# Input projection of a hybrid decoder step: Strassen's seven products in place of the direct one, with the sums of weight blocks formed on GpSimd

## The chip, the core and the metric

The kernel runs on one core of a Trainium2 chip. A core has TensorE (matmuls, out of SBUF into PSUM), VectorE, ScalarE, GpSimd, SyncE (which here only issues DMAs) and 16 DMA engines. The metric is the device time of one execution in microseconds. The engines run their own instruction lists in order and meet at semaphores.

## The reference

One step of a decoder layer, for a prompt of 1024 tokens and 8 samples of 4 tokens (1056 tokens in all). What the change touches is the first line of the layer:

```python
h = rmsnorm(x, norm_g) * (1 + scale[:, None, :]) + shift[:, None, :]
u = h @ w_in        # 1056 x 1024  by  1024 x 6960
# q (1024 columns), three K/V pairs and gates (816), conv h, B, C (1024 each), z (2048)
```

The columns for q, h, B, C and the two halves of z, 6144 of them, are the "input projection" below. From them come `u = cc * hc`, `y_conv = bc * short_conv(u)`, times `silu(z_c)`; `silu(z_a)`; and q. The K/V columns go to the compressed, selected and window attention. Everything is fp32; each fp32 product is made of three products of rounded parts (high x high, high x low, low x high).

## The kernel before

**Stages.** TensorE's list is: the modulation vectors from ada_w (`L997`); the key/value columns, for the samples (`kv_sample`) and then for each of 8 prompt tiles of 128 tokens (`kv(s)`, `L989` to `L991`, 48 matmuls of 384 and 432 columns each); the input projection (`project`, `L1025`); the compression of cached and new keys and values (`turn`, `pair`: transposes `L1069` to `L1071` and matmuls `L1077`, a first pass for keys and a second for values); attention; the output projection (`L1386`).

**The input projection before.** The 6144 columns are 8 groups j of 6 kinds (CC, HC, BC, ZC, ZA, QQ), each 128 columns wide, 48 column groups. The weights wr (1024 x 128, 512 KB) of a group are split by ScalarE into a rounded high part wh (`L1470`) and by VectorE into the low rest wl (`L1775`); the tokens were split once into hhi and hlo (`L1764`). A group is 8 slices of the inner dimension x 3 products (wh hhi, wh hlo, wl hhi) x 3 column chunks of 352 tokens: 72 matmuls, each with its own 128 x 128 weight load, into three PSUM banks; the kinds alternate between two sets of three. ScalarE and VectorE evacuate (cct, uu, yy, zt, ych, zab, qhi, qlo), GpSimd stores mixed, z_attn_silu and q_stacked.

**Order around it.** Every engine's list is written out by hand. SyncE (`load_w`) loads wr two kinds ahead. Before its first load it waits for the store of the bias rows (`row_st`, `L513`, 3 MB). Between the loads stand, one at a time, those for the gate vector (gw, 8 x 512 KB, `L545`, `L548`, `L564`), for the compression's weights (w1, `load_w1`, `L528`, in j = 3) and for the rows of new keys (xp, `load_rows`, `L535` and `L537`, 24 DMAs in j = 4 to 7). The gate products (`gates`, `L1033`) stand between the first kinds. Behind the projection SyncE issues `load_rows(1, r)`, 24 DMAs for the values, and `load_w1(1, q)`. GpSimd gathers the cached keys in quarters of 2 MB (`gather_quarter`, `L781`): the first before the projection, the second right behind it, the others after the last stores and the memset `L814`. `turn(0, 0)` waits for the first quarter and for all 24 row loads (`xp_ld[c]` at 384).

Of the kernel before, what the change touches and what calls it, by code (L numbers as in the profile page):

```python
# [45 lines left out]
NK = 6  # L46
# [11 lines left out]
def build(nc: "bass.Bass", x_prompt, x_sample, cache_k_cmp, cache_v_cmp, cache_k_slc, cache_v_slc, cache_k_win,  # L58
# [27 lines left out]
    with ctx:  # L86
# [3 lines left out]
        zad = nc.dram_tensor("z_attn_silu", [8, P, TOK], F32, kind="Internal").ap()  # L90
        mixd = nc.dram_tensor("mixed", [16, P, TOK], F32, kind="Internal").ap()
# [11 lines left out]
        idxc = sb("idxc", [P, 2], I32)  # L103
        idxq = sb("idxq", [P, 2, 4], I32)
        idxs = sb("idxs", [P, NB], I32)
        pidx = sb("pidx", [P, 2], I32)
        pgc = sb("pgc", [P, 2], I32)
        pgs = sb("pgs", [P, NB], I32)
        sg = sb("sg", [P, NTT, 3 * NH])
        kcs = sb("kcs", [P, NB * NSB])  # L110
        vcs = sb("vcs", [NSB, NB, DKV])
        kcp = sb("kcp", [P, NG, 2 * NPB], F32R)
        sb("apart0", [P, P])
# [4 lines left out]
        kvt = sb("kvt", [P, NTT - 1, KVW], cx=cV)  # L118
# [3 lines left out]

        cH = ExitStack()
        adaw = [sb(f"adaw{i}", [P, 2 * D], cx=cH) for i in range(KC)]
        cH.close()
        cA = ExitStack()
        hhi = sb("hhi", [P, KC, TOK], F32R, cA)
        hlo = sb("hlo", [P, KC, TOK], F32R, cA)

        c0 = ExitStack()  # L130
        vrow = sb("vrow", [31, D], cx=c0)
        relx = sb("relx", [33, NH], cx=c0)
        rel31 = sb("rel31", [32, NH], cx=c0)
# [10 lines left out]
        scale1 = sb("scale1", [P, KC], cx=c0)  # L144
        h32s = sb("h32s", [P, KC, SAMP], cx=c0)
        wkh = [sb(f"wkh{i}", [P, KC, w], F32R, c0) for i, w in enumerate((KV0, KV1))]
        wkl = [sb("wkl0", [P, KC, KV0], F32R, c0)]
        cS = ExitStack()
        adar = sb("adar", [9, 2 * D], cx=cS)
        cS.close()  # L150
        wkl.append(sb("wkl1", [P, KC, KV1], F32R, c0))
        sq = sb("sq", [P, D], cx=c0)
# [2057 lines left out]
```

## Time and profile before

| | |
|---|---|
| median of 3 runs | 1554.61 us (1551.36 to 1560.05) |
| span of the profiled execution | 1556.0 us |
| TensorE busy | 1486.5 us, 96% |
| VectorE, ScalarE, GpSimd busy | 692.7, 621.4, 199.9 us |
| L1025, three kinds of product, 1152 matmuls each | 250.6, 248.3, 248.0 us |
| chain that ended last | TensorE 85% |

The page gives the span of the profiled execution and no time of its own around it. Matmuls overlap, so their busy times exceed the spacing of their starts; what a stage costs is read from the starts. The chain of waits is the work that set the end: a piece of it that becomes shorter shortens the run by as much, until something else is late.

### The profile page before, as it was taken

To read this page: it belongs to the slowest core of one execution; us is meant where nothing else is said; L and a number is where in the kernel's file an instruction comes from. 1 tells how busy PE (TensorE), PEld (TensorE's weight loads), DVE (VectorE), ACT (ScalarE), POOL (GpSimd) and SP (SyncE) were. 2 spreads that over 40 slices of the span, in tenths; PEclk is the share of its full clock that TensorE was granted. 3 is DMA by queue.
4 is the path that set the end of the run, shared out by engine and by line. 5 is a ranking of instruction groups with operands and counts; after the bars stand their busy time and mean duration, and the time that the engine had idled before them with its cause. 6 is when DMAs were issued, how large, how long until landed. Compare 5 with 4: busy or idle time off the path is not lost.

```text
span 1556.0 us, 25222 instructions
## 1 busy us (share of the span) xinstructions
PE 1486.5 (96%) x9878; PEld 1293.1 (83%) x9878; DVE 692.7 (45%) x1790; ACT 621.4 (40%) x1304; POOL 199.9 (13%) x378
## 2 busy tenths in 40 slices
PE   4899999999999999998999998998998999899998
PEld 1799999999999999997777776776776776688886
DVE  2541222323131312216677666666667655653226
ACT  2331111121111111115557777777777765641111
POOL 1100000001102100003011131131131132000000
PEclk8899999999999999999999999999999999999999
DMA  8814343235325243209721121111111019973231
GB/s 334 144 53 164 99 119 96 67 92 125 105 45 163 80 116 86 65 31 312 223 87 30 35 66 42 28 42 42 28 42 42 28 33 362 257 238 95 82 98 35
DMA packets 169061, 164.59 MB, mean 106 GB/s; under 512 B 52780, under 2 KB 150316, under 8 KB 163760
## 3 DMA queue, kind: packets, MB, share of 16 engines
q1 hardware_dynamic: 155136, 97.26, 23.5%
q0 software_dynamic: 13808, 65.73, 12.4%
q8 instruction: 79, 1.29, 0.3%
q14 instruction: 38, 0.31, 0.1%
HBM read 131.27 MB, written 35.83 MB: 107 GB/s over the span
## 4 chain that ended last, share of the span: by engine, by line
PE 85%; DMA 5%; DVE 4%; SPq 3%; ACT 2%; issue 1%; POOL 0%; DVEq 0%; ACTq 0%
PE PS L1025 36%; PE PS L1386 11%; PE PS L1192 8%; PE PS L1157 7%; PE PS L1136 5%; PE PS L1137 3%; PE PS L1077 2%; DMA kb<-in_cache_k_slc,idxs 1%; DMA adaw<-in_ada_w 1%; DMA xb<-in_x_prompt 1%; PE PS L989 1%; PE PS L990 1%; PE PS L991 1%; PE PS L1239 1%; SPq L535 1%
## 5 line engine op out<-in xcount | busy, mean ns | idle before, releaser
L1025 PE MATMUL PS<-hhi,wh 128*128 128x352 f32 x1152 | 250.6, 326 | 0.6 <-ACT kvt L1434 0.6
L1025 PE MATMUL PS<-hhi,wl 128*128 128x352 f32 x1152 | 248.3, 323 | 0.0
L1025 PE MATMUL PS<-hlo,wh 128*128 128x352 f32 x1152 | 248.0, 323 | 0.0
L1025 PEld LDWEIGHTS PS<-hhi,wh 128*128 128x128 f32 x1152 | 195.4, 189 | 4.5 <-issue 3.0
L1556 ACT ACTIVATE pr<-PS,nm 128x640 f32<-128x640 f32 (+7 forms) x256 | 181.2, 709 | 44.5 <-DVE nm L1908 42.1
L1025 PEld LDWEIGHTS PS<-hhi,wl 128*128 128x128 f32 x1152 | 197.8, 188 | 0.0
L1025 PEld LDWEIGHTS PS<-hlo,wh 128*128 128x128 f32 x1152 | 195.6, 188 | 0.0
L1579 ACT ACTIVATE ptt<-PS 128x512 f32<-128x512 f32 x264 | 149.7, 601 | 43.9 <-PE PS L1157 43.6
L1157 PE MATMUL PS<-ident,pr 128*128 128x128 f32 x1056 | 147.4, 274 | 0.0
L1192 PE MATMUL PS<-ptt,kvt 128*64 128x256 f32 x1056 | 137.2, 391 | 0.0
L1775 DVE TENSOR_TENSOR wl<-wr,wh 128x1024 fp32r<-128x1024 f32 x48 | 58.5, 1219 | 168.2 <-ACT wh L1470 167.7
L1157 PEld LDWEIGHTS PS<-ident,pr 128*128 128x128 f32 x1056 | 122.5, 141 | 8.9 <-ACT ptt L1579 0.4
L1470 ACT ACTIVATE wh<-wr 128x1024 fp32r<-128x1024 f32 x48 | 50.6, 1055 | 184.8 <-PE PS L1025 153.5
L1192 PEld LDWEIGHTS PS<-ptt,kvt 128*64 128x64 f32 x1056 | 67.0, 137 | 41.4 <-issue 16.7
L1908 DVE CUSTOM_DVE_ANT_0 PS<-PS,near,nm 128x256 f32<-128x256 f32 x192 | 94.7, 493 | 6.8
L1907 DVE TENSOR_REDUCE nm<-PS 128x1 f32<-128x128 f32 (+5 forms) x128 | 70.5, 551 | 40.1 <-PE PS L1137 39.5
L1136 PE MATMUL PS<-ksh,qb 128*128 128x384 f32 (+3 forms) x192 | 76.6, 401 | 12.0 <-ACT pr L1556 10.5
L1386 PE MATMUL PS<-woh,mh 128*128 128x512 f32 x256 | 79.3, 391 | 0.0
L1386 PE MATMUL PS<-wol,mh 128*128 128x512 f32 x256 | 79.1, 390 | 0.0
L1386 PE MATMUL PS<-woh,ml 128*128 128x512 f32 x256 | 78.8, 389 | 0.0
L1136 PE MATMUL PS<-kwh,qb 128*128 128x384 f32 (+3 forms) x192 | 70.7, 370 | 7.0 <-ACT pr L1556 7.0
L1077 PE MATMUL PS<-xt,w 128*128 128x273 f32 x256 | 72.5, 406 | 4.5 <-DVE xt L1860 3.0
(318 smaller groups left out, 2194.5 us busy)
## 6 DMA issues: line engine op xcount, KB each, us to landing
wr<-in_w_in SPq DMA_DIRECT2D x32, 512.0 KB, 5.9
adaw<-in_ada_w SPq DMA_DIRECT2D x8, 1024.0 KB, 10.1
wr<-in_w_in SPq DMA_DIRECT2D x32, 256.0 KB, 3.8
qb<-q_stacked SPq DMA_DIRECT2D x32, 256.0 KB, 3.1
mr<-mixed SPq DMA_DIRECT2D x16, 512.0 KB, 3.9
mixed<-ych POOLq DMA_DIRECT2D x8, 528.0 KB, 3.4
z_attn_silu<-zab POOLq DMA_DIRECT2D x8, 528.0 KB, 2.9
xb<-in_x_prompt POOLq DMA_DIRECT2D x8, 512.0 KB, 4.8
```

The source lines that it names most:

```text
L1025: ins = pe.matmul(PS[:, bank + c, 0:CH], a[kind % 2][:, k, :], b[:, k, c * CH:(c + 1) * CH], start=(k == 0 and b is hhi and a is wh), stop ...
L1077: ins = pe.matmul(PS[:, 4 + g, 0:CB], w1[c][:, m, :], xt[m // 4 % 2][:, m % 4, g, :], start=(m == 0), stop=(m == 31))
L1136: pe.matmul(PS[:, b0 + c, x:x + m], q, kh[:, g, a:a + m], start=True, stop=False)
L1157: ins = pe.transpose(PS[:, turn_bank(c), h * P:(h + 1) * P], pr[w % 3][:, h, t * P:(t + 1) * P], ident[:, :])
L1192: ins = pe.matmul(PS[64 * g:64 * g + 64, 6, a:a + 2 * P], v, pt[tc % NPT5][:, 2 * g:2 * g + 2, :].rearrange("p j c -> p (j c)"), start=(t ...
L1386: ins = pe.matmul(PS[0:n, b0 + c, :], a[:, k, 0:n], b[k][:, 512 * c:512 * c + 512], start=(k == 0 and a is mh and b is woh), stop=(k == 15 ...
L1470: act.activation(wh[kind % 2][:, :, :], wr[kind % 2][:, :, :], ACT.Copy).then_inc(w_hi, 1)
L1556: act.activation(pr[r][:, h, 0:k], score_cols(b0, w), ACT.Exp, scale=-1.0, bias=nm[:, r, h:h + 1], accum_out=rsum[:, r, h:h + 1]).then_inc ...
L1579: act.activation(pt[tc % NPT5][:, :, :], PS[:, turn_bank(c), :].rearrange("p (h c) -> p h c", h=4), ACT.Copy).then_inc(pt_act, 1)
L1775: dve.tensor_tensor(wl[kind % 2][:, :, :], wr[kind % 2][:, :, :], f32(wh[kind % 2][:, :, :]), ALU.subtract).then_inc(w_lo, 1)
L1907: link(dve.tensor_reduce(low, cols[:, 0:far], AX.X, ALU.min))
L1908: dve.tensor_tensor_reduce(cols[:, far:k], cols[:, far:k], near[:, head_of(u, h), 2 * P - (k - far):2 * P], 1.0, low if far else 3.0e38, A ...
```

## The change

The projection is done in 24 blocks n = 3j + pair; a block has the two kinds of one pair, (CC, HC), (BC, ZC) or (ZA, QQ). The block's product is a 2 x 2 matrix of blocks: the weights are split by kind and by half of the inner dimension, the token matrix by half of the inner dimension and by half of the tokens (H = 528 each). Blocks 0 to 2 are plain, with 8 products; blocks 3 to 23 are "fast", with Strassen's 7. A product is 4 slices x 3 part products x 2 chunks of 264 columns: 24 matmuls (`multiply`).

- The tokens live in `bo[0..6]`, high and low part: four blocks from the start, and five sums, which VectorE (`op_add`, `op_low`), GpSimd (`low_sums`) and ScalarE (`op_high`) form in 20 slices during the plain blocks (PIECES); `bo` 2 and 3 are overwritten by sums at the end.
- The weights: `wr` holds both kinds of a block (2 x 512 KB), loaded when VectorE has made the last low part of the block before. Five of a fast block's seven weight operands are sums or differences of its quarters, formed in fp32 by GpSimd (`added`, 128 x 512, into two buffers wsum), then split by ScalarE (`high`) and VectorE (`low`) into one of five slots wsl. `prepared_at` says at which product which operand is made.
- A fast block's products go through a ring of four PSUM pairs. ScalarE copies products 0 and 1 out; VectorE adds products 2 to 6 onto them (`joined`, two adds each for products 2 to 4).
- The gate products stand in the key/value stage, one behind each tile, with one gw buffer; in front of the first product TensorE waits for ada_ev, VectorE's four additions of gate.
- The compression's w1 and rows are loaded at the end of block 23; the first gather of cached keys starts in block 23, and the second as well. The eight transposes of conv tails come once, behind the projection.
- The layout of z_attn_silu and mixed follows the token halves; q is stored in 8 DMAs per j in place of 4, and mixed and z_attn_silu in 2 each in place of 1.

```diff
+            def multiply(n, k, op, q, first, last):
+                w, b = wsl[(operand0(n) + k) % NSLOT], bo[op]
+                pe.wait_ge(w_lo, operand0(n) + k + 1)
+                for kk in range(HK):
+                    for x, y in ((0, 0), (0, 1), (1, 0)):
+                        for c in range(2):
+                            ins = pe.matmul(PS[:, 2 * q + c, 0:H // 2], w[:, x, kk, :], b[:, y, kk, c * H // 2:(c + 1) * H // 2],
+                                            start=(first and kk == 0 and x == 0 and y == 0), stop=(last and kk == HK - 1 and x == 1))
                 ins.then_inc(p2_mm, 1)
...
             kv_sample()
             for s in range(1, NTT):
                 kv(s)
+                gates(s - 1)
...
+            load_w(0)
+            for k in range(KC):
+                if k:
+                    sp.wait_ge(ada_mm, KC + k)
+                else:
+                    sp.wait_ge(ada_mm, KC)
+                    sp.wait_ge(h_ev, 1)
+                sp.dma_start(gw[:, :], ada3[:, k, 2 * D:3 * D]).then_inc(adaw_ld[k % 4], 16)
+            for n in range(1, NBLK):
+                load_w(n)
+            sp.wait_ge(*made(NBLK - 1, 2))
+            for q in range(4):
+                load_w1(0, q)
+            sp.wait_ge(xz, 1)
+            sp.wait_ge(kc_st, 32)
+            for r in range(4):
+                load_rows(0, r)
...
+            def added(m):
+                n, k = operand_of(m)
+                po.wait_ge(wr_ld, raw_landed(n))
...
+                if sums_to(m) > 2:
+                    po.wait_ge(w_lo, m - 1)
+                po.tensor_tensor(wsum[(sums_to(m) - 1) % 2][:, :, :], raw(*a), raw(*b), op).then_inc(w_sum, 1)
...
+        def prepared_at(n, i):
+            if plain(n):
+                return EARLY_PREP.get((n, i), ())
+            own, following = operand0(n), operand0(n + 1)
+            if i < 3:
+                return (own + 4 + i,)
+            ahead = {5: (following, following + 1), 6: (following + 2, following + 3)}.get(i, ())
+            return ahead if n + 1 < NBLK else ()
```

TensorE at the end of the first prompt tile and the start of the second, before (wkh, wkl: the K/V weights; hhi, hlo: the tokens):

```order
L989 MATMUL PS<-wkh,hhi 128x432
L990 MATMUL PS<-wkl,hhi 128x432
L991 MATMUL PS<-wkh,hlo 128x432
L989 MATMUL PS<-wkh,hhi 128x384 [waits wk_lo,wk_hi,kv_ev,h_lo,h_hi]
L990 MATMUL PS<-wkl,hhi 128x384
```

The same place after (bo: the tokens; gw: a slice of ada_w for the gate; adaw_ld0: its load):

```order
L1221 MATMUL PS<-wkh,bo 128x432
L1243 MATMUL PS<-gw,vcol 9x256 [waits adaw_ld0]
L1243 MATMUL PS<-gw,vcol 9x256 x3
L1219 MATMUL PS<-wkh,bo 128x384 [waits wk_lo,wk_hi,kv_ev,h_lo,h_hi]
L1220 MATMUL PS<-wkl,bo 128x384
```

A gate product, with its wait for gw, now stands between the tiles.

SyncE ahead of the projection, before:

```order
L513 DMA bias_rows<-rows 2048x1x384 [waits tb_ev,wk_ld]
L524 DMA wr<-in_w_in 128x8x128 [waits tb_ev,kv_mm,row_st,wk_lo]
L524 DMA wr<-in_w_in 128x8x128
L524 DMA wr<-in_w_in 128x8x128 [waits w_lo]
L543 DMA gate<-in_ada_b 9x1024 [waits kv_mm]
L545 DMA gw<-in_ada_w 128x1024 x2
```

And after:

```order
L675 DMA bias_rows<-rows 2048x1x384 [waits tb_ev,wk_ld]
L687 DMA wr<-in_w_in 128x8x128 [waits tb_ev,kv_mm,row_st,wk_lo]
L687 DMA wr<-in_w_in 128x8x128
L710 DMA gw<-in_ada_w 128x1024 [waits h_ev,ada_mm]
L710 DMA gw<-in_ada_w 128x1024 [waits ada_mm] x7
L687 DMA wr<-in_w_in 128x8x128 [waits w_lo]
```

The gw loads moved ahead of the second pair of wr, and stay behind the wait for row_st, the store of bias_rows.

SyncE in the last group of the projection and behind it, before (xp from out_p_kc: rows of new keys; from out_p_vc: of new values):

```order
L524 DMA wr<-in_w_in 128x8x128 [waits w_lo]
L535 DMA xp<-out_p_kc 16x8x64 x2
L537 DMA xp<-in_cmp_pe_k 1x8x128
L535 DMA xp<-out_p_kc 16x8x64 x2
L537 DMA xp<-in_cmp_pe_k 1x8x128
L524 DMA wr<-in_w_in 128x8x128 [waits w_lo] x3
```

SyncE behind the last wr load, after (w from in_cmp_w_k: weights of the first compression pass):

```order
L687 DMA wr<-in_w_in 128x8x64 x3
L692 DMA w<-in_cmp_w_k 128x8x128 [waits p2_mm]
L692 DMA w<-in_cmp_w_k 128x8x128 x3
L699 DMA xp<-out_p_kc 16x8x64 [waits kc_st,xz]
L699 DMA xp<-out_p_kc 16x8x64
L701 DMA xp<-in_cmp_pe_k 1x8x128
L699 DMA xp<-out_p_kc 16x8x64 x2
```

The w and xp loads of the first pass now all stand in one piece behind the last wr, and the first waits for a product of block 23.

## Rows read from the trace of the kernel before

**Rows 1.** The page's busy times, shares of the span and instructions.

```profile
PE 1486.5 (96%) x9878; PEld 1293.1 (83%) x9878; DVE 692.7 (45%) x1790; ACT 621.4 (40%) x1304; POOL 199.9 (13%) x378
```

**Rows 2.** The chain that ended last, in time: start us, us, what.

```profile
254.09 69.91 PE PS L1025 x432
324.11 69.91 PE PS L1025 x432
```

**Rows 3.** TensorE's timeline, key/value stage: start us, us, instruction, idle before.

```profile
55.98 0.42 PE L989 MATMUL PS<-wkh,hhi 128*128 128x384 f32 x1
...
72.19 1.97 PE L962 MATMUL PS<-ident,xb 128*128 128x128 f32 x8 [3.53 <-DVE xb L1712]
...
131.24 0.75 PE L1025 MATMUL PS<-hhi,wh 128*128 128x352 f32 x3 [0.62 <-ACT kvt L1434]
```

**Rows 4.** TensorE's timeline, start of the compression.

```profile
697.35 0.38 PE L1069 MATMUL PS<-ident,xp 128*128 128x128 f32 x2
...
715.00 0.33 PE L1069 MATMUL PS<-ident,xp 128*128 128x128 f32 x1 [2.52 <-DMA xq<-in_cache_k_cmp,idxq]
```

**Rows 5.** TensorE's timeline, matmuls of 512 and of 256 columns.

```profile
1439.62 0.62 PE L1386 MATMUL PS<-woh,mh 128*128 128x512 f32 x2
1440.07 0.62 PE L1386 MATMUL PS<-wol,mh 128*128 128x512 f32 x2
...
822.50 0.28 PE L1136 MATMUL PS<-ksh,qb 128*128 128x256 f32 x1
822.62 0.29 PE L1137 MATMUL PS<-ksl,qb 128*128 128x256 f32 x1
```

**Rows 6.** SyncE's timeline: start us, us of issuing, DMA.

```profile
38.58 0.68 SPq L513 DMA_DIRECT2D bias_rows<-rows  x1
74.45 50.38 SPq L524 DMA_DIRECT2D wr<-in_w_in  x3
```

**Rows 7.** DMA issues by line: KB each, median us to landing.

```profile
wr<-in_w_in SPq DMA_DIRECT2D x32, 512.0 KB, 5.9
...
gw<-in_ada_w SPq DMA_DIRECT2D x8, 512.0 KB, 4.1
...
bias_rows<-rows SPq DMA_DIRECT2D x1, 3072.0 KB, 35.8
```

**Rows 8.** Stretches: us, busy by engine, PEclk, DMA share, GB/s.

```profile
72.20:78.20 6.00, 6.00 (x21) 5.91 (x22) 2.77 (x9) 1.32 (x2) 0.54 (x1) 0.50 0.71 226
705.00:740.00 35.00, 30.88 (x188) 25.68 (x187) 22.96 (x54) 21.71 (x52) 11.25 (x11) 1.00 1.01 325
```

**Rows 9.** Groups of VectorE and GpSimd: xcount, busy us, mean ns, idle before.

```profile
L1775 DVE TENSOR_TENSOR wl<-wr,wh 128x1024 fp32r<-128x1024 f32 x48 | 58.5, 1219 | 168.2 <-ACT wh L1470 167.7
...
L1797 DVE SCALAR_TENSOR_TENSOR yy<-uu,vcol,yy 128x1024 f32<-128x1024 f32 x16 | 20.6, 1285 | 0.6
...
L1786 DVE TENSOR_TENSOR uu<-PS,cct 128x1056 f32<-128x1056 f32 x8 | 10.1, 1258 | 67.9 <-PE PS L1025 67.9
...
L1835 DVE TENSOR_TENSOR gate<-PS,gate 9x256 f32<-9x256 f32 x4 | 1.7, 415 | 0.1
...
L880 POOL TENSOR_TENSOR mixs<-mixs,zau 128x256 f32<-128x256 f32 x32 | 23.4, 732 | 4.6
```

**Rows 10.** SyncE's timeline behind the projection.

```profile
708.05 1.24 SPq L535 DMA_DIRECT2D xp<-out_p_vc  x2
...
725.25 4.70 SPq L535 DMA_DIRECT2D xp<-out_p_vc  x2
...
735.90 0.69 SPq L537 DMA_DIRECT2D xp<-in_cmp_pe_v  x1
...
740.68 10.35 SPq L528 DMA_DIRECT2D w<-in_cmp_w_v  x4
```

**Rows 11.** GpSimd's timeline behind the projection.

```profile
706.11 1.84 POOL L814 MEMSET xp<- 128x2048 f32 x1
```

More of the change, by code:

```diff
@@ new lines, in piece, with raw, is_sum, sums_to @@
+        def piece(n, k):
+            return ((0, 1), (1, 1), (0, 0), (1, 0))[k] if plain(n) else {3: (0, 0), 4: (1, 1)}.get(k)
+        def raw(a, k2):
+            return wr[a][:, HK * k2:HK * k2 + HK, :]
+        def is_sum(m):
+            n, k = operand_of(m)
+            return not plain(n) and k not in (3, 4)
+        def sums_to(m):
+            return sum(is_sum(x) for x in range(m + 1))
+        def source(m):
+            n, k = operand_of(m)
+            return wsum[(sums_to(m) - 1) % 2][:, :, :] if is_sum(m) else raw(*piece(n, k))
@@ new lines, in store_za, with store_q @@
+            def store_za(n, half):
+                po.wait_ge(*act_at(n, f"za{half}"))
+                po.dma_start(zad[n // 3, :, half, :], (er if half == 0 and not plain(n) else ca[half])[:, :]).then_inc(zab_st[half], 16)
+            def store_q(n, half):
+                j = n // 3
+                po.wait_ge(*dve_at(n, f"l{half}"))
+                for g in range(2):
+                    own, head, cols = slice(64 * g, 64 * g + 64), 4 * (j // 2) + 2 * g + j % 2, slice(HT * half, HT * half + HT)
+                    for a in range(2):
+                        po.dma_start(f32(qst[head, 64 * a:64 * a + 64, cols]), f32(qp[own, 2 * half + a, 0:HT])).then_inc(q_st, 16)
@@ L1008, in _, with gates @@
             pe.wait_ge(tb_ev, 2)
+            def gates(k):
+                pe.wait_ge(adaw_ld[k % 4], 16 * (k // 4 + 3))
+                for c in range(4):
+                    ins = pe.matmul(PS[32 * c:32 * c + 9, 2, 0:256], vcol[:, k, 0:9], gw[:, 256 * c:256 * c + 256], start=(k == 0), stop=(k == KC - 1))
+                ins.then_inc(ada_mm, 1)
             kv_sample()
@@ new lines, in _ @@
+            pe.wait_ge(ada_ev, 8)
+            for n in range(NBLK):
+                for i in range(products(n)):
+                    if plain(n):
+                        k, op, out = PLAIN[i]
+                        if i < 4 and n:
+                            pe.wait_ge(*emptied(n - 1, former(out)))
+                        multiply(n, k, op, accumulator(n, out), i < 4, i >= 4)
+                    else:
+                        pe.wait_ge(*pair_emptied(n, i))
+                        if n == NPLAIN and i >= 2:
+                            pe.wait_ge(op_lo, {2: 4, 3: 8, 4: 16, 5: 12, 6: 20}[i])
+                        multiply(n, i, FAST[i], ring_pair(n, i), True, True)
@@ L1495, in _ @@
+            for m in range(4):
+                high(m)
             kv_evac(NTT - 1, 0)
```

829 lines of the change are left out of this document (555 added, 274 removed).

## The prediction

> **What bounds the kernel now.** I read the page's shares first: TensorE is busy for 96% of the span, VectorE for 45% [rows 1]. Then the chain that ended last: through the input projection it is TensorE alone, six column groups (432 matmuls) every 70.02 us [rows 2]. So the projection, from 131.24 [rows 3] to 697.35 us [rows 4], 566.1 us, is bound by the number and pitch of its matmuls. 70.02/432 is 162.1 ns for a matmul of 352 columns; 352 columns at 2.4 GHz are 146.7, so about 15 are added to each. The timelines then show what the change touches at both ends of the projection: the key/value stage before it, and the compression stage behind it, where the rows of SyncE are the ones to look at.
>
> **Matmuls.** Before: 48 column groups of 72 matmuls, 3456 x 0.1621 = 560.2 us. After: three blocks of 8 products and 21 of 7, 171 products of 24 matmuls of 264 columns: 4104, more of them and each shorter. The pitch of 264 columns isn't in the trace. Its neighbours: 512 columns start 225 ns apart (213.3 + 12), 256 columns 120 (106.7 + 13) [rows 5], 352 columns 162 (+15). 110 + 14 = 124 ns is my value; the ends are 118 (+8) and 130 (+20). 4104 x 0.124 = 508.9, so **-51.3 us** (-76 to -27). An eighth of the columns goes, but the fixed part grows with the count: at 136.5 ns nothing would be left.
>
> The Trainium skill (TensorE: Matmul & The Clock Gate, Back-to-back issue gap) gives N/2.4 + 2.5 ns at full clock. By that 352 columns would take 149.2, where the trace has 162.1, and 264 would take 112.5; both sides by the rule give a gain of 515.6 - 461.7 = 53.9 us, the new side alone by it 98.5. The trace contradicts it by 13 ns for each matmul.
>
> **The gate products, moved into the key/value stage.** The order shows TensorE's first gate product now right behind the matmuls of the first prompt tile, ahead of the second tile's. It waits for gw. SyncE issues gw behind wr(0), and that behind its wait for the store of the bias rows, which is issued at 38.58 and lands 35.8 us later; the first wr goes out at 74.45 [rows 6]. Two wr loads of 512 KB go first, then gw, whose landing takes 4.1 [rows 7]: 74.45 + about 4 for the wr pair + 4.1 = 82.5 us. Before, the second tile starts at 55.98 [rows 3]. TensorE will stand from there to 82.5: +26.5. Two things come back: the wait of 3.53 us for xb at 72.19, and the stretch at half clock behind it (0.50 granted in 72.20 to 78.20 [rows 8]), 3 us. But the new, longer stand will bring a half-clock stretch of its own, 3 again. 26.5 - 3.5 - 3 + 3 = **+23 us** (19 to 27; the lower end if gw lands 4.1 behind 74.45). The other seven gate loads have a tile's 48 matmuls (over 8 us) over their 4 us, and are hidden. The products themselves cost the same in either place.
>
> Before the first product TensorE now also waits for ada_ev, four VectorE additions of 0.415 us [rows 9] behind the last gate product, 2.1 with the hand-overs, against the 0.62 that it waited for kvt [rows 3]: **+1.4** (0 to 2.5).
>
> **Inside the blocks.** A fast block is 7 x 24 x 0.124 = 20.8 us, a product 2.98. VectorE's instructions of half the width take a little over half of 1.22 and 1.26 us, 0.7 [rows 9]. In the fullest kind (BC, ZC): 7 low parts 4.9, 8 joins 5.6, 4 products 2.8, two conv taps of 1.285 and about 0.5 for their sample parts, 3.1: 16.4 of 20.8. ScalarE has 7 copies and 2 to 4 evacuations of half the width, less. GpSimd's sum isn't in the trace at this width; 256 columns take 0.73 [rows 9], so 512 take 0.73 to 1.46 (1.3 taken): 6.5 of 20.8. So TensorE stays the bound as long as this chain holds: the next block's wr can't be loaded before VectorE has done the last low part of this one (in product 2, about 8 us into the block), two loads of 512 KB take some 8 us (the page has 5.9 for one [rows 7]), the sum, the high and the low part 2.7: 18.7, against a need at 20.8. A margin of 2 us, which a store of GpSimd's in the same microseconds can use up. In the three plain blocks VectorE also forms the 20 slices of operand sums, 2.1 us each, 61 of 71 us in all. I take **+8 us** (0 to 30) for waits here. Queued behind a late low part on VectorE are the joins, and on them waits TensorE for its PSUM banks.
>
> **The start of the compression.** Before, the weights and rows of the first compression pass (w, and xp from p_kc) were fetched one by one through the projection, and the pass began at 697.35 with nothing to wait for. Now SyncE issues all of them from product 2 of the last block on, 4 products = 11.9 us before the end T: four w loads, then 24 row loads, and turn(0, 0) waits for all 24. The same 24 for the second pass took 28.5 us to issue before (708.05 to 736.6): 0.6 to 0.7 us each at first, up to 2.35 later; four w loads took 10.35 us [rows 10]. In that stretch the gathers held the DMA engines, at 325 GB/s and a share of 1.01 [rows 8]. In the changed kernel two gathers of 2 MB go in at the same time as the w loads, and two more about 10 us after T, behind GpSimd's memset, as before (707.9 [rows 11], 10.6 behind 697.35). w: from -11.9 to about 0; rows: 15.5 us at the free pace, to T + 16, the last third against the gathers, landed T + 22. The ends: everything at the free pace, T + 8.5; the pace of the second pass for all, T + 27. Then the pass runs without the waits that it had, 2.52 for xq [rows 4] and some 5 of smaller ones, but starts at half clock (3) and has the tails in front (1): 22 - 8 + 3 + 1 = **+18** (4.5 to 23). The second pass's rows and w follow on SyncE under the first pass.
>
> **Sum.** -51.3 + 23 + 1.4 + 8 + 18 = -0.9. The profiled execution spans 1556.0 us, 1.4 above the median of the runs (1554.61), so 1556.0 - 0.9 - 1.4 = 1553.7: **1554 us**, no change. 0.5%, 7.8 us, is about what a measurement of this kernel can tell from none.
>
> **Rivals.**
> *Faster, partly hidden (0.25).* The pitch is near that of 256 columns, 121 ns (-63.6), the margins in the blocks hold (+4), and the row loads go at the free pace (+4.5): -63.6 + 23 + 1.4 + 4 + 4.5 = -30.7, 1524. For it: the first of the 24 row loads, two in 1.24 us [rows 10]. Against: the DMA share of 1.01 in the stretch that corresponds.
> *Faster, all hidden (0.08).* The change doesn't do what its order says at the gates, since the bias rows land sooner beside other loads: -51.3 + 1.4 + 4 + 4.5 = -41.4, 1513. Against it: 35.8 us for a store that nothing in the change touches.
> *Slower: GpSimd's sums and VectorE's operations exclude each other (0.19).* Price: in the fullest kind 16.4 + 5 x 1.3 = 22.9 against 20.8, 2.1 for each of seven blocks, 15; in the plain blocks 61 + 20 x 1.3 = 87 against 71, 16. With the 8 above dropped: -0.9 - 8 + 31 = +22, 1577. It decides once VectorE's and GpSimd's time together pass 20.8 us in a block. For it speaks that no row of before has a GpSimd addition beside a wide VectorE one from SBUF; against, that VectorE has 4.4 us of room in the block and only such operations lose as meet.
> The Trainium skill (SBUF — State Buffer, SBUF: two separate sides) has it as a rule: a VectorE instruction with two SBUF inputs and a GpSimd one that reads SBUF share a port pair, and one blocks the other for its whole length. The low parts are such instructions; the joins, with one input from PSUM, are not. No row of before shows it.
> *Slower, by the ends (0.08).* Rows landed at T + 27 and wr late in most blocks (+20): -51.3 + 23 + 1.4 + 20 + 23 = +16, 1571.
>
> **Chances.** The forecast 0.40, its own range 1547 to 1562. Faster by over 0.5%: 0.33; within: 0.40; slower: 0.27. The range that leaves out 2 in 10: 1524 to 1582.
>
> **What would show it.** TensorE with one idle stretch of about 26 us from 56 us on, ended by the DMA of gw, and the projection's first product near 160 us. Fast blocks of 20.8 us, 24 matmuls in 2.98. An idle stretch of about 20 us behind the last product, ended by the DMA of xp. Wrong if a block takes over 21.5 us (then see whether VectorE's low parts end with GpSimd's sums), if the pitch is off 124 by more than 3 ns (12 us), or if either stand is missing.

## The result, and the profile after

The changed kernel takes 1611.76 us (median of 4 runs, 1606.85 to 1614.69), the kernel before 1554.54 beside it: a ratio of 1.0364, 95% interval 1.0334 to 1.0394. It is slower by 57 us, where no change was forecast, and outside the range. The profiled execution spans 1609.9 us, 53.9 above the span before.

The page's busy times, with the groups of the product, GpSimd's sum and VectorE's low part (xcount, busy us, mean ns of one, idle before and who ended it), answer to [rows 1, 9]:

```profile
PE 1443.0 (90%) x10526; PEld 1245.7 (77%) x10526; DVE 949.2 (59%) x2181; ACT 699.9 (43%) x1514; POOL 394.1 (24%) x551
...
L1263 PE MATMUL PS<-bo,wsl 128*128 128x264 f32 x4104 | 516.5, 289 | 49.2 <-DVE wsl L2101 37.1
...
L982 POOL TENSOR_TENSOR wsum<-wr 128x512 f32<-128x512 f32 x105 | 139.7, 1337 | 226.5 <-DMA wr<-in_w_in 167.5
L2101 DVE TENSOR_TENSOR wsl<-wsum,wsl 128x512 fp32r<-128x512 f32 x105 | 108.7, 1035 | 110.4 <-ACT wsl L1719 109.9
```

TensorE is busy for 90% instead of 96%: it works less and waits more. GpSimd's sum takes the 1.3 us that were estimated. VectorE's low part of the same width takes 1035 ns on average where 700 was assumed.

TensorE's timeline shows the stands (start us, us, instruction, idle before and its releaser), against [rows 3, 4]:

```profile
81.15 1.04 PE L1243 MATMUL PS<-gw,vcol 128*9 128x256 f32 x8 [26.10 <-DMA gw<-in_ada_w]
...
159.03 72.13 PE L1263 MATMUL PS<-bo,wsl 128*128 128x264 f32 x576 [2.14 <-DVE gate L2270]
231.79 3.19 PE L1263 MATMUL PS<-bo,wsl 128*128 128x264 f32 x24 [0.64 <-ACT ca L1731]
238.65 7.66 PE L1263 MATMUL PS<-bo,wsl 128*128 128x264 f32 x48 [3.67 <-DVE qp L2160]
251.85 13.81 PE L1263 MATMUL PS<-bo,wsl 128*128 128x264 f32 x96 [5.54 <-DVE qp L2160]
...
344.04 6.23 PE L1263 MATMUL PS<-bo,wsl 128*128 128x264 f32 x34 [10.45 <-DVE wsl L2101]
...
441.16 20.66 PE L1263 MATMUL PS<-bo,wsl 128*128 128x264 f32 x168 [0.27 <-DVE wsl L2101]
463.31 0.96 PE L1263 MATMUL PS<-bo,wsl 128*128 128x264 f32 x6 [1.49 <-DVE wsl L2101]
...
756.53 0.66 PE L1303 MATMUL PS<-ident,xp 128*128 128x128 f32 x2 [31.90 <-DMA xp<-in_cmp_pe_k]
```

The span falls into four stages. The projection ends at 722.2; attention begins with the first matmul of L1373, 858.09 after and 807.93 before:

| stage | before | after | difference |
|---|---|---|---|
| to the first product | 131.24 | 159.03 | +27.8 |
| projection | 566.1 | 563.2 | -2.9 |
| compression | 110.6 | 135.9 | +25.3 |
| attention to the end | 748.1 | 751.8 | +3.7 |

So the projection, which was to give back 43 us, gave 2.9. A product without a wait takes 2.92 us, 121.7 ns for each of its 24 matmuls, a fast block 20.44. 4104 x 0.1217 is 499.4 us; the other 63.8 us are waits and half clock behind them. They lie, by the starts of the blocks, thus: 2.7 in blocks 0 to 2, 15.7 in block 3 (36.14 us), 10.7 and 9.3 in blocks 6 and 8 (31.13 and 29.73), and 25.6 in the 18 other fast blocks, 1.4 each on average; 4.4 of the 25.6 are the first products of blocks 7 and 9, at half clock behind the long stands.

**The loop through one block.** A block's weights can be fetched only when the last low part of the block before is made, and its first product needs the fetch, a sum, a high part and a low part; this chain is called the loop below. GpSimd, ScalarE, VectorE and SyncE between the start of block 11 (441.16) and that of block 12 (463.31):

```profile
446.46 1.28 POOL L982 TENSOR_TENSOR wsum<-wr 128x512 f32<-128x512 f32 x1 [0.50 <-DVE wsl L2101]
449.76 0.56 POOL L960 DMA_DIRECT2D mixed<-yy  x1 [2.02 <-DVE yy L2155]
450.35 1.30 POOL L982 TENSOR_TENSOR wsum<-wr 128x512 f32<-128x512 f32 x1
...
452.42 0.69 DVE L2101 TENSOR_TENSOR wsl<-wsum,wsl 128x512 fp32r<-128x512 f32 x1 [2.36 <-ACT wsl L1719]
...
453.14 21.98 SPq L687 DMA_DIRECT2D wr<-in_w_in  x4
...
460.10 2.52 POOL L982 TENSOR_TENSOR wsum<-wr 128x512 f32<-128x512 f32 x2 [8.45 <-DMA wr<-in_w_in]
...
461.42 0.63 ACT L1719 ACTIVATE wsl<-wsum 128x512 fp32r<-128x512 f32 x1 [5.04 <-POOL wsum L982]
...
462.16 1.01 DVE L2101 TENSOR_TENSOR wsl<-wsum,wsl 128x512 fp32r<-128x512 f32 x1 [4.82 <-ACT wsl L1719]
463.39 1.77 DVE L2101 TENSOR_TENSOR wsl<-wsum,wsl 128x512 fp32r<-128x512 f32 x1 [0.22 <-ACT wsl L1719]
```

The block's last sum (450.35) stands on GpSimd behind the store of mixed, which waits 2.02 us for yy. The last low part comes at 452.42, 11.3 us into the block. Only then wr may be loaded (453.14; the row also holds the two loads of the block after it); it lands 7.0 us later, and the sum, the high part, the low part and the product follow: 22.15 us in all, against TensorE's 20.44. The low part that starts at 462.16 is held until GpSimd's second sum ends (460.10 + 2.52 = 462.62) and ends at 463.17: it takes 1.01 us instead of 0.69. The next one, which begins beside the third sum, takes 1.77. The chain of waits puts the 8.4 us of the reload down as "issue"; only the group of GpSimd names the DMA (167.5 us in 20 waits).

**The start of the compression.** SyncE's row, and the DMA queues in 745 to 750 us (packets, MB, share of the 16 engines; q0 carries GpSimd's gathers, q1 SyncE's row loads), against [rows 8, 10]:

```profile
717.21 10.83 SPq L699 DMA_DIRECT2D xp<-out_p_kc  x2
...
q0 software_dynamic: 232, 1.77, 93.7%
q1 hardware_dynamic: 234, 0.06, 5.4%
```

The first pair of row loads is held for 10.8 us behind w, and in these 5 us the queues move as many packets each, 232 against 234, though a gather's packet is 8 KB and a row's 256 B. It is not so throughout: in 722 to 727 us the counts are 243 and 964. The Trainium skill (DMA: Bandwidth & Descriptors, Queues, rings and completion order) says that each DMA engine goes round the queues that it has work for, a packet at a time. Its packet is made of several descriptors and need not be the one that the profile counts, so the 232 and 234 agree with taking turns and don't show the step.

### The profile page after: what moved, and what is told of

The parts are those of the page before. It is cut to its first block, busy times and chain, and to the rows that moved or that the text cites. A ratio compares the mean times of both kernels' runs of the same rounds, so it can differ in the third digit from the quotient of the medians.

```text
span 1609.9 us, 27851 instructions
## 1 busy us (share of the span) xinstructions
PE 1443.0 (90%) x10526; PEld 1245.7 (77%) x10526; DVE 949.2 (59%) x2181; ACT 699.9 (43%) x1514; POOL 394.1 (24%) x551
## 4 chain that ended last, share of the span: by engine, by line
PE 54%; issue 17%; DVE 11%; POOL 7%; DMA 6%; ACT 4%; SPq 2%; DVEq 0%; POOLq 0%; ACTq 0%
PE PS L1623 11%; PE PS L1429 8%; PE PS L1394 7%; POOL wsum L982 5%; PE PS L1373 5%; PE PS L1311 3%; PE PS L1374 3%; PE PS L1263 3%; DVE wsl L2101 2%; DMA bias_rows<-rows 2%; PE PS L1476 1%; PE PS L1219 1%; PE PS L1220 1%; PE PS L1221 1%; SPq L699 1%
## 5 line engine op out<-in xcount | busy, mean ns | idle before, releaser
L1263 PE MATMUL PS<-bo,wsl 128*128 128x264 f32 x4104 | 516.5, 289 | 49.2 <-DVE wsl L2101 37.1
L1263 PEld LDWEIGHTS PS<-bo,wsl 128*128 128x128 f32 x4104 | 512.7, 193 | 53.2 <-issue 42.5
L982 POOL TENSOR_TENSOR wsum<-wr 128x512 f32<-128x512 f32 x105 | 139.7, 1337 | 226.5 <-DMA wr<-in_w_in 167.5
L2101 DVE TENSOR_TENSOR wsl<-wsum,wsl 128x512 fp32r<-128x512 f32 x105 | 108.7, 1035 | 110.4 <-ACT wsl L1719 109.9
L1719 ACT ACTIVATE wsl<-wsum 128x512 fp32r<-128x512 f32 x105 | 66.3, 632 | 245.8 <-POOL wsum L982 245.8
L1373 PE MATMUL PS<-ksh,qb 128*128 128x384 f32 (+3 forms) x192 | 77.1, 403 | 13.5 <-ACT pr L1880 12.0
L1859 ACT ACTIVATE xt<-PS 64x256 f32<-64x256 f32 x128 | 48.5, 379 | 69.9 <-PE PS L1305 67.6
L1373 PE MATMUL PS<-kwh,qb 128*128 128x384 f32 (+3 forms) x192 | 70.6, 370 | 7.0 <-ACT pr L1880 6.8
L1097 POOL TENSOR_TENSOR wide<-rrec,sg 128x256 f32<-128x256 f32 x64 | 39.2, 613 | 143.5 <-DVE rrec L2383 118.3
L2538 DVE TENSOR_TENSOR ml<-mr,mh 128x1024 fp32r<-128x1024 f32 x16 | 19.6, 1226 | 90.3 <-ACT mh L1976 90.3
## 6 DMA issues: line engine op xcount, KB each, us to landing
wr<-in_w_in SPq DMA_DIRECT2D x32, 512.0 KB, 5.2
mr<-mixed SPq DMA_DIRECT2D x16, 512.0 KB, 3.9
xb<-in_x_prompt POOLq DMA_DIRECT2D x8, 512.0 KB, 4.4
```

What stands on the lines that cost most here:

```text
L982: po.tensor_tensor(wsum[(sums_to(m) - 1) % 2][:, :, :], raw(*a), raw(*b), op).then_inc(w_sum, 1)
L1263: ins = pe.matmul(PS[:, 2 * q + c, 0:H // 2], w[:, x, kk, :], b[:, y, kk, c * H // 2:(c + 1) * H // 2], start=(first and kk == 0 and x == ...
L1373: pe.matmul(PS[:, b0 + c, x:x + m], q, kh[:, g, a:a + m], start=True, stop=False)
L2101: dve.tensor_tensor(wsl[m % NSLOT][:, 1, :, :], source(m), f32(wsl[m % NSLOT][:, 0, :, :]), ALU.subtract).then_inc(w_lo, 1)
```

## The experiments

Each run is of the changed kernel with the edit named. "Against changed" is (ratio - 1.0364) x 1554.5 us, uncertain by about 6 us (e7: 10).

| run | edit | median us | ratio to before, interval | against changed |
|---|---|---|---|---|
| e1 | gate products from behind prompt tile 4 on, by half tiles | 1588.02 | 1.0226 (1.0201 to 1.0251) | -21 |
| e2 | window copies at product 6 | 1597.45 | 1.0283 (1.0257 to 1.0309) | -13 |
| e3 | two scratch pairs for all operand sums | 1613.03 | 1.0391 (1.0364 to 1.0418) | +4 |
| e4 | rows ahead of w | 1604.54 | 1.0321 (1.0291 to 1.0350) | -7 |
| e8 | e4, gathers 3 and 4 behind w | 1597.46 | 1.0301 (1.0273 to 1.0329) | -10 |
| e5 | weights' sums on VectorE | 1583.56 | 1.0200 (1.0178 to 1.0222) | -25 |
| e6 | sums left out | 1564.40 | 1.0079 (1.0052 to 1.0106) | -44 |
| e7 | sums formed, not used | 1584.92 | 1.0245 (1.0186 to 1.0303) | -18 |
| e9 | e5, operand sums on VectorE too | 1589.74 | 1.0240 (1.0200 to 1.0280) | -19 |
| e11 | e5, low parts of q earlier | 1584.84 | 1.0188 (1.0161 to 1.0216) | -27 |
| b0 | e1, e2, e8 | 1562.76 | 1.0057 (1.0039 to 1.0075) | -48 |
| b1 | b0, e5 | 1549.37 | 0.9968 (0.9949 to 0.9986) | -62 |
| b2 | b1, e9, gather 2 behind w | 1551.19 | 0.9986 (0.9966 to 1.0007) | -59 |
| b3 | b1, gather 2 behind w, copies waited | 1534.45 | 0.9884 (0.9867 to 0.9900) | -75 |
| b4 | b3, low parts of q earlier | 1534.58 | 0.9880 (0.9864 to 0.9897) | -75 |
| b5 | b3 with GpSimd's sums again | 1555.75 | 1.0006 (0.9988 to 1.0024) | -56 |
| e12 | b3, one of VectorE's two additions out | 1522.87 | 0.9794 (0.9775 to 0.9814) | -89 |

### One wait at a time: e1 to e4, e8

e1:

```diff
                     ins.then_inc(kv_mm, 1)
+                    if 0 <= 2 * s + c - 9 < KC:
+                        gates(2 * s + c - 9)
...
                 kv(s)
-                gates(s - 1)
```

> The gate products are moved back: the first one stands behind the key/value tile 5's first half, the others behind every further half tile, so that TensorE has work while the bias rows are stored. Theory (the stand of 26.46 us in front of the first gate product is added to the path and nothing behind it gives it back): the first product of the projection comes near 135 instead of 159.0 us, the total falls by 22 to 26 us. Rival (the stand only covers something that is late anyway, the weights of block 0, or the operand sums on VectorE): the first product comes earlier, but blocks 0 to 3 give back more than 8 us, total -5 to -15.

Borne out, at the lower end. By the edit's indices the first gate product stands behind the second half of prompt tile 4, at 92.46, with nothing to wait for, and the projection begins at 139.19 instead of 159.03 (135 was expected); blocks 0 to 3 are as long as they were (24.96, 23.36, 24.44, 35.98).

```profile
139.19 3.06 PE L1264 MATMUL PS<-bo,wsl 128*128 128x264 f32 x14 [2.19 <-DVE gate L2271]
```

e2:

```diff
-                    if i == 3 and n in (6, 8):
+                    if i == 6 and n in (6, 8):
```

> The two copies of the window caches, 2 MB each from DRAM to DRAM, are issued by GpSimd at product 6 of blocks 6 and 8 instead of product 3, when the weights of the next block have landed. Theory (the copy fills the DMA queues just as the next block's weights are fetched: 17 and 14.5 us from issue to the first sum instead of 7): blocks 6 and 8 take 22 us instead of 31.1 and 29.7, total -15 to -18 us. Rival (the copy takes 13 us and then hits the weights of the block after it): blocks 7 and 9 become longer by as much, total -0 to -5.

Mostly the theory: block 6 falls to 20.51 us, block 8 to 22.02. But block 9 rises from 22.99 to 26.80, the rival's kind of effect: VectorE waits 6.61 us there for the store of er, which stands behind the second copy; b1 shows the same wait.

e3:

```diff
-            return (er, eg) if x < 12 and x % 2 else ts
+            return (er, eg) if x % 2 else ts
...
+                    else:
+                        dve.wait_ge(op_lo, 20)
                     joined(n, 2, er, ca[1], ALU.subtract)
```

> The last eight of the 20 operand sums alternate between two pairs of scratch buffers (er, eg and ts), as the first twelve do, instead of sharing one. Theory (block 3 is long because each of these sums is a serial round of VectorE, GpSimd, ScalarE and VectorE of 4.6 us, and the low parts of q, on which TensorE waits for its PSUM banks, are queued behind them): block 3 falls from 36.1 to 26 to 30 us, total -6 to -10. Rival (VectorE's own work, or its low parts held up by GpSimd's sums, is the limit there): block 3 stays within 2 us of 36.

A miss in block 3, which grew from 36.14 to 39.03; the total is the same within the noise. With two pairs GpSimd's additions run closer beside VectorE's work, and a low part in block 3 takes up to 3.37 us (2.13 in the changed kernel):

```profile
231.37 3.37 DVE L2099 TENSOR_TENSOR wsl<-wsum,wsl 128x512 fp32r<-128x512 f32 x1 [1.80 <-ACT wsl L1717]
```

The edit also puts VectorE's joins of block 3 behind the last operand sum (`op_lo`). That wait isn't the cause: the join follows the sum without idle time (261.47), and the growth lies before it, in TensorE's stand for qp, 8.15 us instead of 5.54.

e4 and e8 (e8 adds to e4's exchange a wait of GpSimd's):

```diff
+            for r in range(4):
+                load_rows(0, r)
             for q in range(4):
                 load_w1(0, q)
...
+                    if (c, q) == (0, 2):
+                        po.wait_ge(xp_ld[2], 64)
```

> SyncE issues the 24 row loads of the first compression pass ahead of the four loads of its weights w instead of behind them. Theory (the first row load was held for 10.8 us behind w and two gathers, and the last rows landed in the next gathers' stretch): the rows land near 736 to 745 instead of 756.5, the stand of 31.9 us becomes 15 to 22, w comes no later than the first pair needs it; total -8 to -14 us. Rival (the DMA engines are full, so w takes the place of the rows as the last to land): the stand moves from the first transposes to the first pair of matmuls, total -0 to -4.

> As the run with the rows first, and the third and fourth gather of cached keys wait until w of the first pass has landed. Theory (w, on SyncE's queue, starves while GpSimd's gathers hold the DMA engines: the first pair waited 18.1 us for it): w lands near 745, the wait for it falls from 18 to 3 to 7 us and the later gathers are hidden under the pass: total -15 to -20 against the changed kernel. Rival (the gathers are then late for the pass, 22 us behind its start): half of it comes back as waits for xq, total -6 to -10.

TensorE at the start of the compression, e4 and then e8:

```profile
737.26 0.66 PE L1303 MATMUL PS<-ident,xp 128*128 128x128 f32 x2 [12.85 <-DMA xp<-in_cmp_pe_k]
...
756.91 0.48 PE L1304 MATMUL PS<-ident,near 128*128 128x128 f32 x1 [18.14 <-DMA w<-in_cmp_w_k]
```

```profile
735.67 0.66 PE L1305 MATMUL PS<-ident,xp 128*128 128x128 f32 x2 [12.77 <-DMA xp<-in_cmp_pe_k]
744.41 0.47 PE L1306 MATMUL PS<-ident,near 128*128 128x128 f32 x1 [7.22 <-DMA w<-in_cmp_w_k]
```

In e4 the wait mostly moved from the rows to w, as its rival said: w then met the gathers. In e8 both waits together are 20.0 us instead of 31.9. The total gained less than was expected and no wait for xq appeared; by the ratios e8's gain is 10, by the medians 14.

### What GpSimd's sums cost: e5, e6, e7

e5 forms the five sums by VectorE, in one line's exchange of engine (`po.` to `dve.` in `added`), two of them ahead of the joins. e6 and e7 make high and low part from a raw quarter, so the projection's result is another one; in e7 GpSimd still forms every sum, and SyncE waits for the last of a block before it reloads wr.

```diff
-                    act.wait_ge(w_sum, sums_to(m))
+                act.wait_ge(wr_ld, raw_landed(n))
...
-            return wsum[(sums_to(m) - 1) % 2][:, :, :] if is_sum(m) else raw(*piece(n, k))
+            return raw(*piece(n, k)) if not is_sum(m) else raw(*{0: (0, 0), 1: (1, 0), 2: (0, 0), 5: (0, 1), 6: (1, 0)}[k])
```

> The five fp32 sums of weight blocks of every fast block are formed by VectorE, from the same halves into the same wsum buffers, instead of by GpSimd; the operand sums of the tokens stay shared. Theory 1 (the blocks' time is a loop: last low part of the block, reload of wr, sum, high part, low part, first product; in it GpSimd's sum is 1.27 us where VectorE's is 0.7, and the low part behind it is blocked for 0.33 us by GpSimd's second sum, and the last low part comes at 11.3 us into the block because GpSimd's queue and sums stand before it): fast blocks fall from 22.1 to 20.4 to 21 us, total -15 to -25. Theory 2 (the loop is set by the reload alone): blocks stay at 21.5 to 22.2, total within 5 us. Rival against both (VectorE has 16.4 us of work in the fullest kind, with the sums 19.9, and stands in order, so the joins come late and TensorE waits for its PSUM banks): blocks over 22.5 us, total +5 or more.

> The sums of weight blocks are left out altogether: high and low part are made of the first of the two quarters, so the projection's result is another one. Everything else stays. It gives what the sums and all that hangs on them cost. Theory 1 (loop with the sum in it): fast blocks of 20.4 us but for blocks 3, 6 and 8, of which 6 and 8 keep about 8 us of their wait (the window copies); total -30 to -45. Theory 2 (the reload alone sets the loop): blocks of 21 us or more, total -10.

> GpSimd forms the sums as in the changed kernel, at the same points of its list, but nothing reads them: high and low part are made of the first of the two quarters, as in the run without sums. So only what GpSimd's running does to the other engines is left of them. If GpSimd's sum and VectorE's low part exclude each other: the first low part of each block, issued beside two sums of 1.26 us back to back, takes 1.5 to 2.5 us instead of 0.69, VectorE's low parts have a mean of 1.0 or more, and the total is 5 to 20 us above the run without sums. If they do not: means of 0.69, and the two runs agree within 4 us.

The groups of VectorE's low parts, e6 and then e7, and in e7 GpSimd and VectorE where block 12 passes into block 13:

```profile
L2083 DVE TENSOR_TENSOR wsl<-wr,wsl 128x512 fp32r<-128x512 f32 x159 | 105.9, 688 | 93.3 <-ACT wsl L1703 92.8
```

```profile
L2101 DVE TENSOR_TENSOR wsl<-wr,wsl 128x512 fp32r<-128x512 f32 x159 | 159.7, 1028 | 87.4 <-ACT wsl L1720 86.0
...
467.25 4.70 POOL L986 TENSOR_TENSOR wsum<-wr 128x512 f32<-128x512 f32 x3 [6.69 <-DMA wr<-in_w_in]
...
467.86 2.93 DVE L2101 TENSOR_TENSOR wsl<-wr,wsl 128x512 fp32r<-128x512 f32 x2 [1.79 <-ACT wsl L1720]
```

And, in e7's block 12, its last two low parts and the reload of wr:

```profile
457.28 2.37 DVE L2101 TENSOR_TENSOR wsl<-wr,wsl 128x512 fp32r<-128x512 f32 x2
...
459.68 1.04 SPq L689 DMA_DIRECT2D wr<-in_w_in  x2
```

The same 159 instructions with the same data take 688 ns without and 1028 ns with GpSimd's sums running, though nothing reads those sums. So the two engines do exclude each other. It goes the other way too: GpSimd's sums take from 1.25 to 1.76 us.

With the sums only there, e7 is 26 us slower than e6 by the ratios (1.66%; the interval of e7 is wide), 20.5 by the medians and 16.6 in the profiled executions. SyncE's added wait has no part in it: in every fast block the reload goes out 0.03 us behind the last low part. By the starts of the blocks, 15.2 of the 16.6 us lie in blocks 3, 4, 6, 7 and 8, where operand sums or window copies stand as well, and only 1.8 in the thirteen blocks 10 to 22. There the loop reads thus (means, us, worked out from the timelines):

| blocks 10 to 22 | changed | e5 | e6 | e7 | b5 | b3 |
|---|---|---|---|---|---|---|
| last low part done, from the block's start | 11.4 | 11.2 | 8.0 | 11.0 | 11.6 | 11.6 |
| from there to the landing of wr | 6.6 | 6.5 | 6.3 | 6.6 | 6.7 | 6.6 |
| from the landing to the first low part done | 3.15 | 2.18 | 2.46 | 1.92 | 3.14 | 2.18 |
| block | 21.66 | 20.61 | 20.44 | 20.58 | 21.87 | 20.83 |

Unused sums on GpSimd make the last low part 3 us late (e7 against e6), by exclusion alone, and TensorE still hardly waits, since without the sum in it the loop stays under the 20.44 us of the products. With the sums on VectorE (e5, b3) the last low part is as late as with them on GpSimd. What the engine of the sums changes in such a block is the piece behind the landing, 1 us: the sum is 0.6 us longer on GpSimd, and the low part behind it is held for some 0.3 by the second sum.

In e5 low parts take 694 ns, and none of the last 14 blocks takes over 21.03 us. VectorE, at 3.5 us more work in a block, did not become the limit: theory 1, at its upper end, but not for the late last low part that it gave as one of its reasons. In e6 blocks 6 and 8 kept 3.8 and 3.3 us of their wait, not the 8 that were expected.

Instructions of VectorE with an operand in PSUM aren't touched: of the changed kernel's 168 joins none takes over 710 ns, while low parts, with two operands in SBUF, take up to 2132 (min/median/max; one of the five groups of joins):

```profile
L2185 DVE TENSOR_TENSOR ca<-PS,ca x42: 647/707/710, 260.7 to 718.3; 128x528 f32<-128x528 f32 x42
...
L2101 DVE TENSOR_TENSOR wsl<-wsum,wsl x105: 676/693/2132, 223.3 to 713.1; 128x512 fp32r<-128x512 f32 x105
```

That is the Trainium skill's rule (SBUF — State Buffer, SBUF: two separate sides): two SBUF inputs on VectorE and a GpSimd operation that reads SBUF contend for one port pair, which is held for a whole instruction. The trace agrees in both halves of it.

### Together: b0, b1, b3, b5

> The three moves together (gate products by half tiles from tile 5 on, window copies at product 6, rows then w then gathers), with GpSimd's sums kept. If each removes a wait of its own, their gains add up: 23.7 + 14.3 + 14.3 = 52.3 below the changed kernel's 1611.8, so 1559.5. Rival (the waits cover each other): 1565 or more.

> The three moves, and the weights' sums on VectorE. If GpSimd's sums cost what the run with them on VectorE showed (28 us), less what both edits took off blocks 6 and 8: 1559.5 - 28 + about 4 = 1535, faster than the kernel before by 1%. If their cost is hidden once the moves are made: as the run with the moves alone, 1555 to 1560.

The gains of the three moves add up within the noise (b0, 48 of 21 + 13 + 10). b1 missed by 14 us. In it block 6 still takes 29.75 us and block 9 25.56. GpSimd's and VectorE's rows:

```profile
295.41 0.63 POOL L927 DMA_DIRECT2D out_s_kw<-in_cache_k_win  x1
...
376.50 0.71 DVE L2175 TENSOR_TENSOR er<-PS,ca 128x528 f32<-128x528 f32 x1 [8.25 <-DMA z_attn_silu<-er]
```

The sums had been what held GpSimd's list in step with the blocks. Without them the first copy goes out 10.7 us into block 6, just ahead of the reload; and the store of er, queued behind the second copy, holds VectorE for 8.25 us in block 9. b3 names the moment instead:

```diff
-                    if i == 3 and n in (6, 8):
+                    if i == 6 and n in (6, 9):
+                        po.wait_ge(wr_ld, raw_landed(n + 1))
+                        po.wait_ge(*made(n, 4))
```

> As the run with the three moves and the weights' sums on VectorE, but each window copy is issued by GpSimd in blocks 6 and 9 after a wait for the next block's weights to have landed and for product 4, and the second gather stands behind w. In the run before it GpSimd, with no sums left to hold it back, had issued the first copy early (block 6 kept its 29.75 us), and the second copy had the store of z_attn_silu behind it in its queue, for which VectorE waited 8.25 us in block 9 (25.6 us). Theory: blocks 6 and 9 take 20.4 to 21.5 us, the start of the compression 4 us less; total 1549.4 - 8.5 - 4 - 4 = 1533, range 1530 to 1538. Rival (the copies hit other blocks, where they stand now): 1543 or more.

> The fastest version so far (1534.45 us) with one thing undone: the weights' sums are GpSimd's again. If GpSimd's sums cost what they cost alone (28 us) less the share that lay in the wait for the window copies: 1552 to 1560. If they cost only the blocked low parts on the path (0.33 us a block, 7 in all): 1541.

Both borne out: blocks 6 and 9 take 20.52 us, and b3, at 1534.45, is faster than both kernels, by 1.2% than the one before (interval 1.0 to 1.3). The sums' engine alone makes 19 us of it (b5 against b3, 1.22%), and decides; b5's second alternative, that only the held low parts cost, 7 us in all, is ruled out: with the sums on GpSimd and all else mended, the seven products only draw level with the direct projection. b3's page:

```profile
PE 1434.7 (94%) x10526; PEld 1238.1 (81%) x10526; DVE 961.3 (63%) x2286; ACT 699.0 (46%) x1514; POOL 255.2 (17%) x446
...
L1253 PE MATMUL PS<-bo,wsl 128*128 128x264 f32 x4104 | 509.0, 287 | 15.8 <-DVE wsl L2091 5.8
```

### Block 3: e9, e11, b2, b4, e12

> As the run with the weights' sums on VectorE, and the low halves of the 20 operand sums of the tokens are formed by VectorE too (20 more additions of 0.7 us there, 20 of 1.3 us less on GpSimd), so GpSimd does no arithmetic in the projection. Theory (in the plain blocks and block 3 VectorE loses more by GpSimd's additions, to being blocked and to waiting for them, than the additions cost it): block 3 falls from 32.9 to 27 to 31 us, total 1578 to 1582 where the run before it had 1583.6. Rival (VectorE's own work is the limit in block 3): block 3 becomes longer, 34 us or more, total 1585 or more.

> As the run before it, with the operand sums' low halves on VectorE as well, and the second gather of cached keys also behind w. Theory: block 3 2 to 5 us shorter, w and rows 2 to 4 us earlier: 1528 to 1533. Rival (VectorE is the limit in block 3, or the second gather comes late for the pass): 1536 or more.

A miss, and the rival both times: with 20 more additions VectorE made block 3 35.99 us (32.87 in e5), and b2 is no better than b1 (block 3 36.08). e11 and b4 form the low parts of q, on which TensorE waits in block 3, a product earlier:

```diff
-                    if kind == 2 and i == 1:
+                    if kind == 2 and i == 0:
                         query_low(n, 0, acc(n, C21), samples_of(n, C21))
```

> The same edit alone on top of the run with the weights' sums on VectorE (1583.6 us, block 3 of 32.9): by the theory block 3 takes 27 to 30 and the total is 1578 to 1581; by the rival both stay within 1.5 us.

> As the run before it; VectorE forms the low parts of q of block 2 one product earlier in its list, ahead of an operand sum (and ScalarE the one high part that it needs), since TensorE waits for just these in block 3 (2.4 and 5.1 us). Theory (block 3's loss is the order on VectorE, not its load): block 3 falls from 33 to 27 to 30 us, total 3 to 6 us below the run before it. Rival (VectorE's load: the operand sums come late by what the low parts come early): block 3 within 1.5 us of 33, the wait is for op_lo instead.

The rival again, twice: block 3 takes 33.46 and 33.38 us. Its waits merely moved to other products. e12 takes work away instead:

```diff
-                link(dve.tensor_tensor(t[0][:, :], f32(bo[a][:, 0, x % 4, :]), f32(bo[b][:, 0, x % 4, :]), op))
                 dve.wait_ge(low_sum, 1 + x + 1)
-                dve.tensor_tensor(t[0][:, :], t[0][:, :], t[1][:, :], ALU.add).then_inc(op_sum, 1)
+                dve.tensor_tensor(t[0][:, :], f32(bo[a][:, 0, x % 4, :]), f32(bo[b][:, 0, x % 4, :]), op).then_inc(op_sum, 1)
```

> The fastest version so far with VectorE's second addition of each of the 20 operand sums left out (the token sums lack their low halves, so the projection's result is another one): 20 x 0.71 = 14 us less work for VectorE in blocks 0 to 3, of which 8 sums, 5.7 us, stand in its list where block 3 waits. Theory (VectorE's load sets block 3): block 3 falls from 32.9 to 26 to 29 us, total -4 to -7. Rival (the hand-overs between VectorE, GpSimd and ScalarE set it): block 3 stays within 2 us.

TensorE in block 3, b3 and then e12:

```profile
215.59 3.18 PE L1253 MATMUL PS<-bo,wsl 128*128 128x264 f32 x24 [1.05 <-DVE qp L2150]
220.93 4.70 PE L1253 MATMUL PS<-bo,wsl 128*128 128x264 f32 x24 [2.15 <-ACT ca L1721]
230.09 20.15 PE L1253 MATMUL PS<-bo,wsl 128*128 128x264 f32 x143 [4.47 <-DVE qp L2150]
```

```profile
219.53 11.93 PE L1253 MATMUL PS<-bo,wsl 128*128 128x264 f32 x96 [0.94 <-DVE qp L2149]
234.48 5.75 PE L1253 MATMUL PS<-bo,wsl 128*128 128x264 f32 x34 [3.01 <-DVE wsl L2091]
```

Block 3 falls from 32.91 to 24.80 us, and the total by 14 (12 by the medians), both by more than was expected. More additions make it longer, fewer make it shorter, another order leaves it: VectorE's list of operand sums sets it. The weights' sums on GpSimd add 3.0 to 4.5 us there (b5 against b3 35.95 and 32.91, e7 against e6 34.71 and 30.17). The edit takes away a hand-over with the addition, so how much of the 8 us is the one and how much the other stays open.

## Why the prediction was wrong

**Matmuls: -51.3 forecast, -60.8 measured** (499.4 against 560.2). The pitch is 121.7 ns where 124 was taken, inside its ends: 110 + 11.7, the fixed part of the 512 columns, not the 14 chosen between neighbours. The rule that the prediction quotes for the gap stands in the Trainium skill (TensorE: Matmul & The Clock Gate, Back-to-back issue gap) for a matmul by itself, not for a stream in which each matmul has its weight load; so the 13 ns that the trace has above it were no contradiction.

**Gate products: +23 and +1.4 forecast, +23.4 measured.** The step was right: from start to start the stand is 26.46 us, 26.10 of them idle (26.5 forecast), ended by the DMA of gw, and the first product came at 159.03 (near 160). Of the 27.8 us by which it is late 4.4 are the gate products themselves, which took 4.4 us inside the projection before; e1 got back 21 (by the medians 24).

**Inside the blocks: +8 (0 to 30) forecast, 62 measured** (63.8, less the 1.5 us that the projection before had beside its matmuls and gate products). This is the step that failed, and it alone puts the time outside the range. It failed in four places.
- The loop. The last low part was put at 8 us into the block and starts at 9 to 12.5. The 8 us are right for a kernel without sums (e6). Either engine that forms the sums makes it 3 us later: GpSimd by holding VectorE's instructions (e7), VectorE by forming them itself (e5). In block 11 the store that waits for yy, in front of GpSimd's last sum, is on the path too. With 7.0 us for the reload (8 was taken) and 3.1 from the landing to the low part (2.7) the loop is 22.15 us there, not 18.7. Over the 18 ordinary blocks the waits are 25.6 us.
- The window copies. "A store of GpSimd's in the same microseconds can use up" the margin named it, but no store was looked for, its size least of all: 2 MB, twice, 20 us. e2 got 13 of it back, and in b3 the blocks with the copies take 20.52 us.
- Block 3, 15.7 us. The plain blocks' load on VectorE was counted (61 of 71 us), the waits between the pieces of a sum were not, nor that the lag would be paid in block 3.
- Exclusion. The rival's mechanism is shown (e7); it was priced at 31 us with a chance of 0.19. Its rule, VectorE's and GpSimd's time together over 20.8 us in a block, was not what decided: in ordinary blocks exclusion alone costs TensorE 0.1 us each (e7), and it costs more where operand sums or copies have used up the margin. Moving the sums to VectorE gave 25 us alone and 19 with all else mended; in ordinary blocks that is 1 us each, of which some 0.3 is the held low part.

**Start of the compression: +18 (4.5 to 23) forecast, +25.3 measured.** The place and the releaser were right. The rows landed at T + 34, not T + 22: the free pace of 0.65 us a load was right once they ran, but the first pair was held for 10.8 us behind w, and the last landed 12 us after its issue, beside the next gathers, where 6 had been allowed. The sum let w be through by T; its price for the two gathers beside w was nothing, though the text names them.

**Sum.** The measured terms make -60.8 + 23.4 + 62.3 + 25.3 + 3.7 = 53.9, the difference of the spans; the 3.7 are attention and what follows, which the prediction left at nothing. Of the 55 us that the forecast missed, 54 are the blocks' term, 7 the compression's and 4 the last stage's; the matmuls gave 9.5 back and the gates 1. The rivals "slower" priced the blocks at 20 and 31 us; in the blocks four sources of waiting held at once.

## What to carry to other kernels

When a faster arithmetic leaves TensorE a margin of 2 us in a block, write the whole loop down (last use of the buffer, reload, each engine's hand-over) and, beside each step, what stands before it in that engine's list and queue. A sum on GpSimd isn't free because GpSimd is idle: it took twice as long as on VectorE (1337 and 685 ns), and it held VectorE's instructions with two operands in SBUF. What cost TensorE was not the holding by itself, which a block with room took without loss (e7), but mostly the longer sum and the held low part in the one chain that had no room: 19 us for 105 sums (b5 against b3). Work that keeps an engine in step is a hidden wait: when it is taken away, name the moment of every DMA that stood behind it.

## What the runs showed of the hardware that was not expected

- Two DMA queues can move as many packets each while one moves thirty times the bytes: 232 packets of a gather carried 1.77 MB in the 5 us in which 234 of the row loads carried 0.06 MB.
- A GpSimd sum beside a low part doesn't slow it but blocks it to the sum's end: 0.69 us alone, 1.77 beside one sum, 2.93 for two beside three sums (1.28 for two in the run without sums).
- The clock behind short stands. In blocks 4 to 23 of the changed kernel the granted clock fell to 0.50 around the stands of 10.45 and 9.05 us (338.0 to 348.2 and 392.6 to 402.8) and behind those of 2.24 and 2.58 us (508.7 to 512.0 and 638.4 to 641.7); the first products there take 4.3 to 5.4 us instead of 2.92. Behind six other stands, of 1.4 to 2.3 us, they take 3.0. So the length of a short stand alone doesn't tell. The mean over these blocks is 0.97 (268 to 722.2 us), and 1.00 over the same blocks of b3.
